# Two weight sums of each pair and the last residual add, moved from VectorE into transfers that add

## The reference, cut to what matters

```python
x = x + rmsnorm(jnp.einsum('btd,de->bte', mix, w_o), g_post_mix)

hf = rmsnorm(x, g_pre_ff)
ff = jnp.einsum('btf,fd->btd', jnp.square(jax.nn.relu(jnp.einsum('btd,df->btf', hf, w_ff1) + b_ff1)), w_ff2) + b_ff2
x = x + rmsnorm(ff, g_post_ff)
```

## Time and profile before

| | us |
|---|---|
| median of 3 runs (1226.82 to 1227.23) | 1226.94 |
| the profiled execution | 1226.39 |
| its span, first to last instruction | 1224.8 |
| PE busy | 1200.2 (98%) |
| DVE busy | 866.0 (71%) |
| ACT busy | 544.0 (44%) |
| POOL busy | 65.4 (5%) |

### The profile page before, as it was taken

One profiled execution on the slowest core, in us unless ns is written; L12 is line 12 of the kernel. 1 busy time (PEld: TensorE's weight loads), 2 busy tenths in 40 slices (PEclk: granted clock), 3 DMA queues, 4 the chain that ended last, 5 costly groups with the idle time before them and its releaser, 6 DMA issues.

```text
span 1224.8 us, 22983 instructions
## 1 busy us (share of the span) xinstructions
PE 1200.2 (98%) x8893; PEld 1128.2 (92%) x8893; DVE 866.0 (71%) x1275; ACT 544.0 (44%) x836; POOL 65.4 (5%) x129
## 2 busy tenths in 40 slices
PE   9999999999999999999999999999999999999995
PEld 9999978989797898879999999999999999999994
DVE  6933788988888898887455434338687587585897
ACT  7533443453454345435543222246655453454543
POOL 4020001101100110110000000000000000000000
PEclk9999999999999999999999999999999999999998
DMA  6354226516432651623223232432433233333332
GB/s 222 104 160 147 70 71 222 199 34 224 170 130 69 222 199 34 239 105 104 87 86 88 85 97 74 158 105 67 145 104 104 87 87 104 87 93 98 86 125 73
DMA packets 44680, 145.95 MB, mean 119 GB/s; under 512 B 4756, under 2 KB 7188, under 8 KB 44232
## 3 DMA queue, kind: packets, MB, share of 16 engines
q1 hardware_dynamic: 33048, 103.74, 26.6%
q0 software_dynamic: 11424, 41.23, 9.6%
q10 hardware_dynamic: 144, 0.09, 0.0%
HBM read 120.54 MB, written 24.49 MB: 118 GB/s over the span
## 4 chain that ended last, share of the span: by engine, by line
PE 94%; DVE 3%; ACT 1%; issue 1%; DVEq 0%; POOL 0%; ACTq 0%; POOLq 0%
PE product L2051 73%; PE side L2051 21%; DVE yacc L2041 0%; PE side L2236 0%; ACT yacc L1294 0%; DVE yacc L1942 0%; ACT hhi L1159 0%; ACT cq L1139 0%; DVE hlo L1878 0%; DVE yacc L2045 0%; ACT whi L765 0%; DVE wlo L1916 0%; DVE wlo L1917 0%; DVE common L1942 0%; DVE wlo L1923 0%
## 5 line engine op out<-in xcount | busy, mean ns | idle before, releaser
L2051 PE MATMUL product<-ahi,whi 128*128 128x272 f32 x1232 | 261.7, 292 | 2.8 <-DVE cq L1860 1.6
L2051 PE MATMUL product<-ahi,wlo 128*128 128x272 f32 x1232 | 256.9, 288 | 0.0
L2051 PE MATMUL product<-alo,whi 128*128 128x272 f32 x1232 | 256.9, 288 | 0.0
L1322 DVE TENSOR_TENSOR wlo<-wraw,whi 128x1024 fp32r<-128x1024 f32 x122 | 148.8, 1224 | 114.5 <-ACT whi L765 102.6
L765 ACT ACTIVATE whi<-wraw 128x1024 fp32r<-128x1024 f32 x122 | 127.9, 1054 | 199.3 <-PE product L2051 121.7
L2051 PEld LDWEIGHTS product<-ahi,whi 128*128 128x128 f32 x1232 | 194.8, 188 | 13.1 <-issue 12.3
L2051 PEld LDWEIGHTS product<-alo,whi 128*128 128x128 f32 x1232 | 194.6, 189 | 0.0
L2051 PEld LDWEIGHTS product<-ahi,wlo 128*128 128x128 f32 x1232 | 193.7, 189 | 0.0
L1535 DVE SCALAR_TENSOR_TENSOR accp<-u,wdw,accp 128x512 f32<-128x512 f32 x240 | 163.7, 745 | 0.7 <-DVE accp L1535 0.7
L2051 PE MATMUL side<-hhi,whi 128*128 128x272 f32 x252 | 73.0, 290 | 3.6 <-DVE yacc L1942 1.4
L2051 PE MATMUL side<-hlo,whi 128*128 128x272 f32 x252 | 72.5, 288 | 0.0
(11 more groups left out here) (348 smaller groups left out, 2464.8 us busy)
## 6 DMA issues: line engine op xcount, KB each, us to landing
wraw<-in_wstream SPq DMA_DIRECT2D x176, 512.0 KB, 3.7
crg<-in_c_in POOLq DMA_DIRECT2D x32, 512.0 KB, 6.7
out_c_s<-crg POOLq DMA_DIRECT2D x32, 512.0 KB, 3.2
hb<-head_rows POOLq DMA_DIRECT2D x4, 580.0 KB, 5.3
x<-in_xT SPq DMA_DIRECT2D x4, 544.0 KB, 6.5
sgm<-in_xT SPq DMA_DIRECT2D x1, 2176.0 KB, 9.3
x_rows<-yc SPq DMA_DIRECT2D x1, 2176.0 KB, 10.1
x1b<-x_rows SPq DMA_DIRECT2D x1, 2176.0 KB, 9.5
```

The lines of the kernel that those rows point to most:

```text
L1322: V.tensor_tensor(wlo[:, k % RING, :, :], wraw[:, k % 2, :, :], whi[:, k % RING, :, :].bitcast(f32), ALU.subtract).then_inc(lo_done, 1)
L2051: return pe.matmul(out, lhsT, rhs, start=start, stop=stop, skip_group_check=check)
```

## The change

Two of the four sums of a pair are no longer made by DVE. SP loads a quarter of the second chunk into the place of S1 as well, and POOL issues two transfers per pair that add what they bring from memory onto what lies in SBUF: a11 onto a21 (this gives S3), and a22 onto the copy of a21 in S1's place. DVE keeps S2 and S4. ACT's first split waits for the transfer of S3, DVE's S2 for that of S1. The first pair's S1 gets a place of its own, `first_s1`, in a part of `yacc` that is not yet in use.

The residual is stored to the output itself at first, and no longer loaded again. The four last stores, now issued by POOL, add the scaled result onto what lies in the output.

```diff
-SUMS = 4
+SUMS = 2
...
+        first_s1 = at("first_s1", [P, KT // 2, P], f32, free_ + (KT - 2) * TT * 4)
...
+        def s1_of(d):
+            return s1[d % 2] if d > 0 else first_s1
...
             sp.wait_ge(x1_ready, 2 * KT)
-            sp.dma_start(x1_dram, yc[:, :, :]).then_inc(x1_moved, 16)
+            sp.dma_start(yT, yc[:, :, :]).then_inc(x1_moved, 16)
...
+                if is_down(t):
+                    d = order_of(t)
+                    if d == 1:
+                        sp.wait_ge(chunk_done, C_FF + KT)
+                    if d > 1:
+                        sp.wait_ge(split_lo, SPLIT_AT[DOWNS[d - 2], "sums"])
+                    sp.dma_start(s1_of(d)[:, :, :], wstream[two, :, 0:KT // 2, :]).then_inc(s1_in[d % 2], 16)
...
-            product_of(sp, WHEN["down", GROUPS - 2, IN_GROUP - 1], "P3")
-            sp.wait_ge(x1_moved, 16)
-            sp.dma_start(x1b[:, :, :], x1_dram).then_inc(x1_moved, 16)
...
-                    sp.wait_ge(out_dve, 2 * g + half + 1)
-                    sp.dma_start(yT[:, tiles, part], yacc[:, tiles, part]).then_inc(out_saved, 16)
...
+            for d, t in enumerate(DOWNS):
+                one, two = chunks_of(t)
+                pool.wait_ge(first_in[t % 2], first_due(t))
+                pool.dma_start(raw_of(t)[:, 0, KT // 2:KT, :], wstream[one, :, 0:KT // 2, :], accum_op=ALU.add).then_inc(s3_in[d % 2], 16)
+                pool.wait_ge(s1_in[d % 2], 16 * (d // 2 + 1))
+                pool.dma_start(s1_of(d)[:, :, :], wstream[two, :, KT // 2:KT, :], accum_op=ALU.add).then_inc(s1_sum[d % 2], 16)
+            pool.wait_ge(x1_moved, 16)
+            for g in range(2):
+                part = slice(HALF * g, HALF * (g + 1))
+                for half in range(2):
+                    tiles = slice(KT // 2 * half, KT // 2 * (half + 1))
+                    pool.wait_ge(y_scaled, 2 * g + half + 1)
+                    pool.dma_start(yT[:, tiles, part], yacc[:, tiles, part], accum_op=ALU.add).then_inc(out_saved, 16)
...
                 if is_down(t):
-                    act.wait_ge(sum_made, SUMS * order_of(t) + 2)
+                    act.wait_ge(s3_in[order_of(t) % 2], 16 * (order_of(t) // 2 + 1))
...
-                dve.wait_ge(second_in[t % 2], first_due(t))
-                if d < 2:
-                    dve.wait_ge(chunk_done, C_FF + KT)
-                else:
-                    dve.wait_ge(split_lo, SPLIT_AT[DOWNS[d - 2], "sums"])
-                V.tensor_tensor(sum_1, a21, a22, ALU.add).then_inc(sum_made, 1)
-                dve.wait_ge(sum_made, n + 1)
-                V.tensor_tensor(a21, a21, a11, ALU.add).then_inc(sum_made, 1)
+                dve.wait_ge(s1_sum[d % 2], 16 * (d // 2 + 1))
...
-            dve.wait_ge(x1_moved, 32)
...
-                for half in range(2):
-                    tiles = slice(KT // 2 * half, KT // 2 * (half + 1))
-                    dve.wait_ge(y_scaled, 2 * g + half + 1)
-                    V.tensor_tensor(yacc[:, tiles, part], yacc[:, tiles, part], x1b[:, tiles, part], ALU.add).then_inc(out_dve, 1)
```

More of the change, by code:

```diff
@@ L352, in hybrid_layer @@
         assert u0 + 2 * form_ + quarter_ <= u0 + KT * TT * 4 and u0 + 2 * form_ + quarter_ <= tmp0 - 4 * quarter_
-        x1b = at("x1b", [P, KT, TT], f32, tmp0)
         free_ = tmp0 + 6 * form_
@@ L362, in hybrid_layer @@
         s1 = [at(f"s1_{n}", [P, KT // 2, P], f32, ring_at + (8 * n + 7) * quarter_) for n in range(2)]
-        x1_dram = nc.dram_tensor("x1_rows", (P, KT, TT), f32, kind="Internal").ap()
+        first_s1 = at("first_s1", [P, KT // 2, P], f32, free_ + (KT - 2) * TT * 4)
         psum = [ctx.enter_context(nc.psum_tensor(f"product{s}", [P, 2, 512], f32)) for s in range(2)]
@@ L432, in hybrid_layer @@
         bank_read = {eng: sem(f"bank_read_{eng}") for eng in _reads}
+        s1_in = [sem(f"s1_in{s}") for s in range(2)]
+        s3_in, s1_sum = ([sem(f"{n}{s}") for s in range(2)] for n in ("s3_in", "s1_sum"))
         cq_pos, cq_squared, tt_made, form_hi, form_lo = (sem(n) for n in (
@@ L437, in hybrid_layer @@
         tail_stat, tail_root = sem("tail_stat"), sem("tail_root")
-        y_scaled, out_dve = sem("y_scaled"), sem("out_dve")
+        y_scaled = sem("y_scaled")
         block = ctx.enter_context(nc.Block())
@@ L612, in _ @@
                 unit_load(t)
-            product_of(sp, WHEN["down", GROUPS - 2, IN_GROUP - 1], "P3")
-            sp.wait_ge(x1_moved, 16)
-            sp.dma_start(x1b[:, :, :], x1_dram).then_inc(x1_moved, 16)
-            for g in range(2):
-                part = slice(HALF * g, HALF * (g + 1))
-                for half in range(2):
-                    tiles = slice(KT // 2 * half, KT // 2 * (half + 1))
-                    sp.wait_ge(out_dve, 2 * g + half + 1)
-                    sp.dma_start(yT[:, tiles, part], yacc[:, tiles, part]).then_inc(out_saved, 16)
             sp.wait_ge(out_saved, 16 * 4)
@@ L1175, in sums_split @@
                 act.activation(whi[:, 1, 0:KT // 2, :], s2[:, :, :], ACT.Copy)
-                act.activation(whi[:, 1, KT // 2:KT, :], s1[order_of(t) % 2][:, :, :], ACT.Copy).then_inc(split_hi, 1)
+                act.activation(whi[:, 1, KT // 2:KT, :], s1_of(order_of(t))[:, :, :], ACT.Copy).then_inc(split_hi, 1)
             def second_split(t):
@@ L1888, in sums_made @@
                 a11, a21, a12, a22 = (raw[:, n // 2, KT // 2 * (n % 2):KT // 2 * (n % 2 + 1), :] for n in range(4))
-                sum_1, n = s1[d % 2][:, :, :], SUMS * d
+                sum_1, n = s1_of(d)[:, :, :], SUMS * d
                 dve.wait_ge(first_in[t % 2], first_due(t))
-                dve.wait_ge(second_in[t % 2], first_due(t))
-                if d < 2:
-                    dve.wait_ge(chunk_done, C_FF + KT)
-                else:
-                    dve.wait_ge(split_lo, SPLIT_AT[DOWNS[d - 2], "sums"])
-                V.tensor_tensor(sum_1, a21, a22, ALU.add).then_inc(sum_made, 1)
-                dve.wait_ge(sum_made, n + 1)
-                V.tensor_tensor(a21, a21, a11, ALU.add).then_inc(sum_made, 1)
+                dve.wait_ge(s1_sum[d % 2], 16 * (d // 2 + 1))
                 if d > 0:
@@ L1916, in sums_low @@
                 V.tensor_tensor(wlo[:, 1, 0:KT // 2, :], s2[:, :, :], whi[:, 1, 0:KT // 2, :].bitcast(f32), ALU.subtract)
-                V.tensor_tensor(wlo[:, 1, KT // 2:KT, :], s1[order_of(t) % 2][:, :, :], whi[:, 1, KT // 2:KT, :].bitcast(f32),
+                V.tensor_tensor(wlo[:, 1, KT // 2:KT, :], s1_of(order_of(t))[:, :, :], whi[:, 1, KT // 2:KT, :].bitcast(f32),
                                 ALU.subtract).then_inc(split_lo, 1)
```

## The result

The changed kernel takes 1230.87 us (median of 7 runs) against 1226.94 for the kernel before: ratio 1.0035, 95% interval 1.0024 to 1.0047. It is slower by 0.35%, where 1224.6 was forecast. The profiled execution took 1230.93 us, with a span of 1229.4.

A forecast was written before the change was run, and what follows sets the result against it. PE was taken to bound the whole kernel, DVE two units and the tail. The sums' -4.4 us and the tail's +2.1 gave -2.3, so 1224.1 against the profiled execution and 1224.6 as median; range 1219.3 to 1231.

The forecast's parts named there:

- The sums' relief: Two sums leaving DVE shorten PE's waits in units 11, 22 and 23: -4.4 us, between -2.5 and -5.8.
- Unit 11's wait: PE's wait at 1029.95 us goes, 0.33 idle and 0.16 more: 0.5 us won.
- units 22 and 23: PE's two units that wait for DVE, losing 5.3 us: unit 23 ends at 1171.05 instead of 1174.94, 3.9 us won.
- The waits that I named as next late: Unit 23 after the change: forms cost P1 about 0.5 us and P7 about 0.6, the add of P5 0.3.
- The first pair: No gain: its sums lie ahead of an instruction that waits for ACT in any case.
- The sums as transfers: Loads and POOL's adds cost nothing on the path: 12 us of slack for an add of 256 KB.
- The residual: Four last stores add in the transfer, taking 11.5 us; DVE loses four adds of 1.2 us; tail +2.1 us.
- The tail: The kernel's end after PE, with the adding stores and POOL's drain: +2.1 us, between -3.2 and +9.2.
- 1.64 + 0.2 + 0.95: Around the last stores' transfers: 1.64 us fixed per store, 0.2 for POOL's issue, 0.95 from landing to POOL's drain end.
- sign that the forecast named for being wrong: Forecast wrong if the stores' rate lies outside 170 to 220 GB/s, or PE waits for a transfer in any pair.
- two passes: Likeliest case: adding stores read, then write, 11.5 us at about 190 GB/s; 1224.6 us, chance 0.45.
- three passes: Rival: adding stores read, add and write without overlap, 18.6 us at 120 GB/s; tail +9.2, 1231.7 us, chance 0.19.

The follow-up runs named there:

- the larger space: The changed kernel with 5120 instead of 4096 bytes per partition set aside for the descriptors of POOL's transfers: 1227.29 us, ratio 1.0002 to the kernel before.
- the plain stores: The changed kernel with its four last stores, issued by POOL, replacing instead of adding, which leaves the residual out: 1220.79 us, ratio 0.9944 to the kernel before.
- the long rows: The changed kernel with each adding store covering two whole tiles (256 rows of 2176 bytes) instead of four half tiles (512 of 1088): 1230.06 us, ratio 1.0019.
- the sums alone: The kernel before with only the two sums made by transfers, the residual as before: 1223.85 us, ratio 0.9971; again 1223.00 us, ratio 0.9964.
- the sums left out: Sums by transfers and the old tail, but both adding transfers of a pair left out, so the two sums are not made: 1223.19 us, ratio 0.9969.
- one add on POOL: Sums by transfers and the old tail, but the first of four residual adds is a POOL instruction instead of DVE's: 1225.12 us, ratio 0.9980.

## Why the prediction was wrong

**The sums' relief: right, 3.8 of 4.4.** Unit 11's wait is gone and gave 0.57 where 0.5 was said (from the chain's first unit to 1034.69: 111.56 us before, 110.99 after). In units 22 and 23 it gave 3.2 of 3.9. The waits that I named as next late are there at their sizes: the forms at 1160.86 and 1162.98 cost 0.45 and 0.63 (said: 0.5 and 0.6), the add of P5 at 1170.13 0.33 (0.3). Two I had missed. In unit 22 P3 waits for the add of P5 too, 0.27 at 1157.81. In unit 23 P4 waits for the add of P7, 0.44 at 1168.30, because DVE paused ahead of it (DVE in time order, changed kernel):

```profile
1165.97 0.69 DVE L1910 TENSOR_TENSOR s<-s,wraw 128x512 f32<-128x512 f32 x1
1167.16 0.69 DVE L1915 TENSOR_TENSOR s<-wraw,s 128x512 f32<-128x512 f32 x1 [0.50 <-DVE s L1910]
1167.77 0.43 DVE L1951 TENSOR_TENSOR yacc<-yacc,product 128x272 f32<-128x272 f32 x1
```

S4 follows S2 after 1.19 us, where in the pair before it is 0.82 (1153.97 to 1154.79). It does so in the run without the adding transfers as well. Why is open. The first pair is unmoved, as said.

**The sums as transfers: right.** No wait on the path, shown by the run that leaves them out. The slack was smaller than the 12 us said, most of all for S1: in the changed kernel S3 lands 8.4 us or more ahead of the ACT split that reads it, S1 4.7 or more ahead of DVE's S2. DVE's busy time fell by 24 us (866.0 to 841.8), 26 were said.

**The residual: wrong, and this decided the sign.** The failed step is "I add 0.2 because POOL's issue takes 0.54 us against SP's 0.375": four issues were taken for four short instructions that nothing stops. The tail was forecast 2.1 us longer and is 7.8 longer. Of the 5.7 us between, 3.1 are the hold of the fourth store: that is what the larger space gives back (21.3 to 18.2). Another 1.8 are the beginning and the end of the four transfers. In the run with the larger space POOL begins 1.2 us behind the first scale's end, the first bytes move 1.9 us later, and the span ends 1.5 us behind the last ones: 4.6, where I had 1.64 + 0.2 + 0.95 = 2.8. And 0.8 is the rate: the bytes take 12.3 us there, 11.5 were said. Why the beginning and the end take 1.8 us more is open.

The larger space shows what each part decided. With the hold gone the change is neither faster nor slower, 1.0002 (0.9993 to 1.0012): these 2.6 us and the 0.6 of relief that didn't come had used up the 2.3 us of gain, and the hold then made it slower. Neither sign that the forecast named for being wrong, another rate or a matmul waiting for a transfer, appeared; a store that is held back was in none of its rivals.

The size of two passes was right: 191 GB/s, within the 170 to 220 that the forecast set as its bound, and 0.56 of the plain stores' 342. The rule of halving in the Trainium skill, "Collectives: The Full Stack", section "The bandwidth ceiling: the fold count and why AG ≠ RS ≠ AR", agrees roughly; an estimate by that page, half of its 31 GB/s of an engine on 16 engines, would be 248 GB/s, which no adding store here reached (189 to 193, and 202 with the long rows).

The result, 1230.9, lies close to the rival of three passes, 1231.7, and that is an accident: three passes would be 120 GB/s without a hole, and the trace shows 191 with one. A rival's time alone doesn't tell that the rival was right.

**The sign of it stood in the trace of before.** POOL's loads of the convolution's history near the start, kernel before (start, us, what, idle before):

```profile
11.95 2.83 POOL L671 DMA_DIRECT2D u<-in_hist  x3 [4.47 <-DMA x<-in_xT]
18.54 2.65 POOL L671 DMA_DIRECT2D u<-in_hist  x3 [3.76 <-issue]
24.33 1.76 POOL L671 DMA_DIRECT2D u<-in_hist  x2 [3.15 <-issue]
```

Each has 128 x 8 = 1024 rows of 120 bytes. Three go out, then POOL waits 3.76 us for nothing that the profile shows, three more, and again. Here too each wait ends 0.35 us behind the landing of the third and of the sixth (18.20 and 23.99). An adding store of 512 rows behaves as a plain transfer of 1024: two entries for each row. 3072 entries fit in 4096 bytes, 4096 entries don't, and in 5120 bytes they do. The history loads, the adding stores of 512 and of 256 rows, the plain stores and the larger space all fit this. That an adding row takes two entries is inferred from these counts, not shown by itself; they allow any number between 1.5 and 2.7. Packets are not what fills the space: the three history loads have 96, the four stores with long rows 512 and no hold. Had I read "issue" ahead of a repeated transfer as a wait for room, the term would have been in the sum: about 3 us, 1227.7 instead of 1224.6, and no gain.

## What to carry to other kernels

In these runs a transfer that adds took work off an engine for nothing only where it had slack, as the sums do with 4.7 us or more of it. At the kernel's end, where transfers are the last thing, it moved little more than half as fast as a plain one, took, by the counts above, twice the descriptor entries, and over 1.5 times the issue time. Before several transfers are put on POOL's queue, count rows times reads against the space set aside for descriptors, and look in the trace for POOL waiting on "issue" between transfers of one kind; where it does, see whether the wait ends with the landing of the last one issued. When a change has two independent halves, price and run them apart: here one won 3.8 us and the other lost 7.8.

## What the runs showed beyond that

- DVE's add of two operands from SBUF took 3.45 us instead of 1.2 beside a POOL add of the same kind (3.38 us), while DVE's two scales just ahead of it (1209.28, 2.49 us for both) kept their 1.2. The Trainium skill, "SBUF — State Buffer", section "Terms", says that DVE and POOL arbitrate for one pair of ports, held for a whole instruction, and that the loser stands still; the add agrees with it. The second scale, which ran until 1211.77, tells nothing against it, as it had started at 1210.48, ahead of POOL's 1210.72; whether POOL's 3.38 us hold a wait for it, no run here shows.
- Adding stores with rows of 2176 bytes moved 202 GB/s, with rows of 1088 bytes 189 to 193.
- In three traces (the first run of the sums alone, the sums left out, one add on POOL) PE's last steps ahead of the tail took 1.6 us more at the same work. The granted clock tells why; the sums left out, then the sums alone in the second run:

```profile
1202.00:1206.00 4.00, 2.21 (x7) 1.48 (x8) 1.08 (x3) 3.86 (x8) 0.00 (x0) 0.89 0.00 0
1206.00:1210.00 4.00, 3.73 (x17) 3.06 (x15) 0.69 (x2) 1.46 (x4) 0.00 (x0) 0.68 0.00 0
```

```profile
1202.00:1206.00 4.00, 2.17 (x9) 1.54 (x9) 1.13 (x3) 3.90 (x8) 0.00 (x0) 1.00 0.00 0
1206.00:1210.00 4.00, 3.01 (x17) 2.03 (x16) 2.27 (x3) 2.98 (x7) 0.00 (x0) 1.00 0.00 0
```

It is 0.89 and 0.68 against 1.00 (the columns after the busy times); 1.00 is the level of 2.4 GHz and 0.50 that of 1.2. PE had been busy for 2.2 of 4 us in both, so why the clock fell in the one alone is open. The sums alone show both in their two traces, so the kernel alone doesn't decide it; the tails in the table begin behind it.
